# S5 tap masks as one VectorE product per window, with a changed order of the mixer's work

## Chip, cores and metric

One core of one Trainium2 chip runs the whole program in one launch. The metric is the device time of that launch in microseconds (us), and the median of several runs is compared. TensorE is the matmul engine, VectorE and ScalarE are the two elementwise engines, GpSimd is the slower general one, and SyncE issues most of the DMAs. In the profile they are called PE, DVE, ACT, POOL and SP.

## What is computed

One inference step of a hybrid decoder layer for 256 prompt tokens and 8 samples of 8 tokens (320 token columns in all, T = 320). The mixer at the layer's start has two halves that share one input projection: an S5 state-space group (512 channels, here "u") and an RWKV-7 group (the projections r, k, v and z, 512 channels each). After it come cross-attention and a top-4-of-32 mixture of experts. The change touches the S5 half alone:

```python
def s5_mixer(u, h0_re, h0_im, lam_re, lam_im, log_dt, b_re, b_im, c_re, c_im, d, glu_w, glu_b):
    dt = jnp.exp(log_dt.astype(f32))[:, None]
    mag = jnp.exp(lr * dt)
    ar = mag * jnp.cos(li * dt)
    ai = mag * jnp.sin(li * dt)
    ...
    bu_r = jnp.einsum('btgc,gpc->btgp', uf, bbar_r)
    bu_i = jnp.einsum('btgc,gpc->btgp', uf, bbar_i)
    acc_r, acc_i, x_r, x_i = lax.associative_scan(_complex_affine_combine, (a_r, a_i, bu_r, bu_i), axis=1)
    ...
    y = (jnp.einsum('gcp,btgp->btgc', c_re.astype(f32), x_r)
         - jnp.einsum('gcp,btgp->btgc', c_im.astype(f32), x_i)
         + d.astype(f32).reshape(S5_NGROUPS, S5_GROUP) * uf)
    z = jax.nn.gelu(y)
    out = z * jax.nn.sigmoid(z @ glu_w.astype(f32) + glu_b.astype(f32))
```

## The kernel before, in words

The recurrence is cut into blocks of BL = 8 tokens (40 blocks in 320 columns). The 512 S5 channels are handled in four tiles of 128 channels, numbered 0 to 3, and each tile goes through the same steps:

- **load** (`load_windows`, ScalarE's DMA queue): eight DMAs of 160 KB, one for each tap, gather shifted copies of u from DRAM into a window buffer of 128 x 2560 numbers (8 taps of 16 channels on the partitions, 8 groups of 320 columns along them). There are two buffers, for the even and the odd tiles. From tile 2 on, the load waits for the block matmuls of the tile two before.
- **win** (`mask_windows`, L1408 to L1413): a tap that reaches back beyond the start of its block of 8 has to be zero. ScalarE multiplies the window in place, one instruction for each of 7 column positions of the block, each 128 x 320 elements with a mask column as its scale.
- **f**, **par** (`f_matrices`, `s5_params`): the input matrices, made on VectorE for tiles 0 and 1 and on GpSimd for tiles 2 and 3 (L1701 to L1706, six products), then transposed by TensorE (L742) and multiplied to a kernel matrix (L746, L747), and copied out by ScalarE (L1350, L1397, L1398). GpSimd's six products for tile n+2 wait until TensorE has done `kk` of tile n+1, and they stand behind its own scan and start steps of tile n.
- **blk** (`s5_block`): TensorE's two jobs on the masked window, the block ends (L760) and the local part (L767). It waits for the masks (semaphore `uwin`).
- **scan** (L1894 to L1905, VectorE), after ScalarE has copied the block ends. GpSimd then forms the start state of every block (L1716 to L1726, the last of them signals `s5_x0`).
- **y** (L1909), **c** (L1879 to L1883, the output matrices; two rounds of two products and two halves), **out** (`s5_out`, L779 on TensorE, waits for the start states and the output matrices), **gelu** (L1914 to L1917; the first of the three frees the PSUM bank of `out`) and **gated** (L1922).

Between these steps TensorE computes the 16 tiles of the RWKV input projection (**in** k0 to v3, L716, 16 passes of 128x320 for a tile with two of them in each 1 MB weight chunk), and VectorE the token-shift mixing of them: **mix** (L1835 to L1844), **delta** and **shares** for z. Weight chunks for these tiles come over SyncE's queue into three slots in turn (L557). A chunk's load starts when TensorE has finished the last job that read the slot's former chunk: the chunk of r2 and r3 is requested when z1 is done.

The order of all that is a list written out by hand, `MIX_ORDER`. Every engine walks through the same list and does the steps that are its own, in that order, so a step waits on its own engine for everything ahead of it. PSUM banks go round by eight over the jobs in list order.

Of the kernel before, what the change touches and what calls it, by code (L numbers as in the profile page):

```python
# [25 lines left out]
ACT = mybir.ActivationFunctionType  # L26
# [11 lines left out]
BL = 8  # L38
# [137 lines left out]
def _tiles(kind, name, lo, hi):  # L176
# [2 lines left out]

IN_ORDER = "kzrv"  # L180
MIX_ORDER = [("in", "k0"), ("memsum", 0), ("load", 0), ("in", "k1"), ("f", 0), ("in", "k2"), ("load", 1), ("c", 0), ("in", "k3"),
             ("par", 0), ("memtotal", 0), ("win", 0), ("in", "z0"), ("f", 1), ("blk", 0), ("scan", 0), ("y", 0), ("in", "z1"), ("load", 2),
             ("memroot", 0), ("mix", "k"), ("in", "z2"), ("win", 1), ("out", 0), ("par", 1), ("in", "z3"), ("c", 1), ("blk", 1), ("gelu", 0),
             ("scan", 1), ("gated", 0), ("y", 1), ("in", "r0"), ("load", 3), ("delta", "z"), ("in", "r1"), ("shares", 0), ("shares", 1),
             ("out", 1), ("par", 2), ("c", 2), ("in", "r2"), ("win", 2), ("blk", 2), ("shares", 2), ("scan", 2), ("y", 2), ("gelu", 1),
             ("gated", 1), ("in", "r3"), ("in", "v0"), ("mix", "r"), ("out", 2), ("par", 3), ("in", "v1"), ("win", 3), ("c", 3), ("gelu", 2),
             ("gated", 2), ("blk", 3), ("scan", 3), ("y", 3), ("lora_up", 0), ("in", "v2"), ("in", "v3"), ("kk", 0), ("memnorm", 0),
             ("out", 3), ("gelu", 3), ("mix", "v"), ("gated", 3), ("lora_down", 0), ("knorm", 0), ("decays", 0), ("memk", 0),
             ("decay_exp", 0), ("memk", 1), ("memk", 2), ("memk", 3), ("memk", 4), ("memk", 5), ("glu", 0)]
TILES4 = range(4)  # L190


# [133 lines left out]
def build(nc, a, o):  # L326

    with ExitStack() as ctx:
# [5 lines left out]
        def S(name):  # L334
            if name not in sems:
                sems[name] = ctx.enter_context(nc.semaphore(name))
            return sems[name]
# [15 lines left out]
        def con(name, lo=0, hi=P):  # L353
            at, n = CON[name]
            return BIG[lo:hi, CONO + at:CONO + at + n]
# [11 lines left out]
        def over(ap, axis, n):  # L367

            v = ap.unsqueeze(axis)
            shape = list(v.shape)  # L370
            shape[axis] = n
            return v.to_broadcast(shape)
# [307 lines left out]
        def _(pe):  # L680
# [68 lines left out]

            def s5_block(ct):  # L750

                pe.wait_ge(S("uwin"), (BL - 1) * (ct + 1))
                uwin = uwins[ct % 2]
                stored(pe, f"ei{ct}")
                b = start_job(f"ve{ct}")
                for q in range(PAIRS):
                    for g in range(2):
                        for ri, e in ((0, E_r), (1, E_i)):
                            at = (ri * PAIRS + q) * NBL
                            last = mm(b[64 * g:64 * g + 64, at:at + NBL], e[:, q, 64 * g:64 * g + 64],  # L760
                                      uwin[:, 2 * q + g, BL - 1::BL], start=True, stop=True)
                end_job(last, f"ve{ct}")
                stored(pe, f"kk{ct}")
                b = start_job(f"loc{ct}")
                for g in range(2):
                    for q in range(PAIRS):
                        last = mm(b[32 * q:32 * q + 32, 0:T], kkz[:, 2 * q + g, :], uwin[:, 2 * q + g, :],  # L767
                                  start=(g == 0), stop=(g == 1))
                end_job(last, f"loc{ct}")
# [575 lines left out]
        def _(act):  # L1345
# [59 lines left out]
                    src = bass.AP(u_dram, ct * P * (T + 7) + tap, [[T + 7, GC], [GC * (T + 7), 8], [1, T]])  # L1405
                    act.dma_start(uwins[ct % 2][tap * GC:(tap + 1) * GC], src).then_inc(S(f"uwin_in{ct % 2}"), 16)

            def mask_windows(ct):  # L1408

                act.wait_ge(S(f"uwin_in{ct % 2}"), 16 * BL * (ct // 2 + 1))  # L1410
                w = uwins[ct % 2].rearrange("p g t -> p (g t)")
                for j in range(BL - 1):
                    step(af(w[:, j::BL], w[:, j::BL], ACT.Identity, scale=con("window")[:, j:j + 1]), "uwin")  # L1413

            act.wait_ge(S("u_stored"), 16)
            act.wait_ge(S("consts_in"), 16)
            for kind, n in MIX_ORDER:
                if kind == "in":
                    copy(prj[n[0]][:, int(n[1]), :], n)
                elif kind == "par":  # L1420
                    s5_params(n)
                elif kind == "load":
                    load_windows(n)
                elif kind == "win":
                    mask_windows(n)
                elif kind == "memsum":
                    norm_parts(rm, "m")
                elif kind == "memroot":
                    norm_roots(rm, "m", "rm")
                elif kind == "blk":  # L1430
                    if n >= 2:
                        act.wait_ge(S("s5_x0"), n - 1)
                    else:
                        act.wait_ge(S("s5_tables"), 1)
                    copy(xes[n % 2], f"ve{n}", lambda b: b[:, 0:2 * PAIRS * NBL].rearrange("p (r q n) -> p r q n", r=2, q=PAIRS))
                elif kind == "gelu":
                    act.wait_ge(S("gelu_arg"), n + 1)
                    step(af(mix[:, n, :], mix[:, n, :], ACT.Tanh, scale=float(np.sqrt(2 / np.pi))), "gelu_tanh")
                elif kind == "lora_up":
                    for job, dst, rows, fn in (("lw", hidden["dw"], 64, ACT.Tanh), ("la", hidden["da"], 64, ACT.Identity),  # L1440
                                               ("lg", hidden["dg"], P, ACT.Sigmoid)):
                        b = computed(act, job)
                        step.read_out(af(dst[0:rows, :], b[0:rows, 0:T], fn), job)
                elif kind == "lora_down":
                    for i in TILES4:
                        b = computed(act, f"dw{i}")
                        step.read_out(af(R[3][:, i, :], b[:, 0:T], ACT.Sigmoid, bias=vec("rwkv_w0", i)), f"dw{i}")
                    act.wait_ge(S("delta_free"), 1)
                    for i in TILES4:
                        b = computed(act, f"da{i}")  # L1450
                        step.read_out(af(R[7][:, i, :], b[:, 0:T], ACT.Sigmoid, bias=vec("rwkv_a0", i)), f"da{i}")
                    for i in TILES4:
                        copy(R[5][:, i, :], f"dg{i}")
                elif kind == "decay_exp":
                    act.wait_ge(S("decay_sums"), 1)
                    step(af(R[12], R[13], ACT.Exp, scale=-DECAY), "decay_exps")
                    step(af(R[9], R[13], ACT.Exp, scale=DECAY), "decay_exps")
                elif kind == "memk":
                    copy(mkT[:, n, :], f"mk{n}", lambda b: b[:, 0:NM])
                elif kind == "knorm":  # L1460
                    stored(act, "kn3")
                    inverse_root(R[15], R[15], 1.0, None, "kk_norm")
                elif kind == "glu":
                    for i in TILES4:
                        b = computed(act, f"gl{i}")
                        step.read_out(af(view(UWIN, CT, T)[:, i, :], b[:, 0:T], ACT.Sigmoid, scale=0.5, bias=vec("s5_glu_b", i)), f"gl{i}")
# [270 lines left out]
        def _(dve):  # L1737
# [147 lines left out]
            def scan_blocks(ct):  # L1885
# [18 lines left out]
                step(tt(xp[:, 0], xp[:, 0], turned[:, 0], sub))  # L1904
                step(tt(xp[:, 1], xp[:, 1], turned[:, 1], add), "s5_scanned")  # L1905

            def s5_local(ct):
                b = computed(dve, f"loc{ct}")
                step.read_out(stt(yl[ct], uT[:, ct, 7:], vec("s5_d", ct), b[:, 0:T], mul, add), f"loc{ct}")  # L1909
# [74 lines left out]
            for kind, n in MIX_ORDER:  # L1984
                if kind == "mix":
                    mixes(n)
                elif kind == "delta":
                    delta(n)
                elif kind == "shares":
                    share("z", R[4 + n], 3 + n)  # L1990
                elif kind == "memnorm":
                    mem_norm()
                elif kind == "f":
                    f_matrices(n)
                elif kind == "c":
                    c_matrices(n)
                elif kind == "y":
                    s5_local(n)
                elif kind == "scan":
                    scan_blocks(n)  # L2000
                elif kind == "gelu":
                    s5_gelu(n)
                elif kind == "gated":
                    s5_gated(n)
                elif kind == "kk":
                    kk_squares()
                elif kind == "decays":
                    decays()
# [368 lines left out]
```

## Time and profile before

| | us |
|---|---|
| median of 3 runs | 1464.74 |
| lowest and highest of them | 1461.38, 1467.27 |
| the profiled execution: its time | 1463.18 |
| the profiled execution: its span, first to last instruction | 1461.4 |
| TensorE busy | 1372.5 |
| VectorE busy | 436.1 |
| ScalarE busy | 266.0 |
| GpSimd busy | 54.6 |

The span is the stretch that every view of the trace covers, with its zero at the first instruction. The stretch of the S5 tiles and the projections lies at the start of it, from 29 us to about 176 us; the RWKV part and the attention follow, and the expert stage runs from about 520 us to the end. In the timeline a row is a run of equal instructions of one engine: start, duration to the end of the last, engine, line, operation, tiles, count, and in brackets the idle time before it with what ended it.

### The profile page before, as it was taken

How to read it: one execution, taken by the hardware profiler on the slowest of the kernel's cores; microseconds unless marked ns; L12 is line 12 of the kernel's file. 1: busy time of each engine (PE TensorE's matmuls, PEld its weight loads, DVE VectorE, ACT ScalarE, POOL GpSimd, SP SyncE). 2: the span in 40 equal slices, each digit the busy share in tenths (PEclk: the TensorE clock that was granted, in tenths of full speed). 3: DMA queues.
4: the chain of work that ended last, by engine and by line, in shares of the span. 5: the costliest groups of instructions: out<-in, count | busy, mean ns of one | idle time of the engine just before them, and what ended most of it. 6: DMA issues, size and time to landing. Idle time of an engine off the chain costs nothing.

```text
span 1461.4 us, 21175 instructions
## 1 busy us (share of the span) xinstructions
PE 1372.5 (94%) x8649; PEld 695.2 (48%) x8649; DVE 436.1 (30%) x879; ACT 266.0 (18%) x494; POOL 54.6 (4%) x111
## 2 busy tenths in 40 slices
PE   8796999999999999999999999998998999988997
PEld 5564688866665633434334343343343433433442
DVE  5787746435121221312112111121121111311112
ACT  4344331212223112101101011011010110110102
POOL 4342000000000000000000000000000000000000
PEclk9898999999999999999999999999999999999999
DMA  8871021013839679999999999999999999999994
GB/s 324 159 158 60 30 93 60 32 59 120 353 140 409 277 264 398 404 424 427 428 427 428 428 428 428 428 427 429 428 427 429 428 428 428 429 427 427 426 426 166
DMA packets 43335, 471.84 MB, mean 323 GB/s; under 512 B 4992, under 2 KB 10368, under 8 KB 11520
## 3 DMA queue, kind: packets, MB, share of 16 engines
q1 hardware_dynamic: 37264, 461.42, 76.1%
q10 hardware_dynamic: 6000, 9.41, 3.3%
q8 instruction: 52, 0.85, 0.2%
q14 instruction: 19, 0.16, 0.0%
HBM read 465.33 MB, written 5.48 MB: 322 GB/s over the span
## 4 chain that ended last, share of the span: by engine, by line
PE 71%; DMA 20%; DVE 4%; ACT 3%; issue 2%; ACTq 1%; SPq 0%; DVEq 0%
DMA big<-in_w_gu 18%; PE bank L1186 16%; PE bank L1235 14%; PE bank L716 9%; PE bank L1109 5%; PE bank L796 2%; PE bank L976 2%; PE bank L1299 2%; PE bank L1255 2%; ACT big L1413 2%; PE bank L895 1%; DMA big<-u_windows 1%; PE bank L1116 1%; PE bank L1211 1%; PE bank L1284 1%
## 5 line engine op out<-in xcount | busy, mean ns | idle before, releaser
L1186 PE MATMUL bank<-big 128*64 128x512 f32 x1920 | 427.9, 602 | 28.3 <-DMA big<-in_w_gu 27.3
L1186 PEld LDWEIGHTS bank<-big 128*64 128x64 f32 x1920 | 147.0, 138 | 306.1 <-issue 295.8
L1235 PE MATMUL bank<-big 128*64 128x512 f32 x960 | 209.4, 594 | 0.0
L716 PE MATMUL bank<-big 128*128 128x320 f32 (+1 forms) x688 | 187.8, 430 | 3.1 <-ACT big L1521 1.3
L716 PEld LDWEIGHTS bank<-big 128*128 128x128 f32 x688 | 130.1, 191 | 58.0 <-issue 8.1
L2232 DVE TENSOR_TENSOR big<-big,bank 128x320 f32<-128x320 f32 x120 | 58.5, 487 | 304.2 <-PE bank L1255 298.9
L2218 DVE TENSOR_SCALAR big<-bank 128x512 f32<-128x512 f32 x32 | 22.2, 693 | 392.5 <-PE bank L1186 362.3
L1235 PEld LDWEIGHTS bank<-big 128*64 128x64 f32 x960 | 69.9, 137 | 128.2 <-issue 126.5
L1590 ACT ACTIVATE big<-big 128x512 f32<-128x512 f32 x30 | 18.8, 626 | 449.3 <-DVE big L2218 449.3
L1350 ACT ACTIVATE big<-bank 128x320 f32<-128x320 f32 (+3 forms) x122 | 53.2, 436 | 222.9 <-PE bank L716 45.4
L1109 PE MATMUL bank<-big 128*128 128x512 f32 x192 | 85.4, 593 | 1.4 <-DVE big L2166 1.4
L1255 PE MATMUL bank<-big 128*128 128x320 f32 x240 | 68.9, 439 | 0.0
L1255 PEld LDWEIGHTS bank<-big 128*128 128x128 f32 x240 | 44.1, 189 | 28.9 <-issue 12.2
L1109 PEld LDWEIGHTS bank<-big 128*128 128x128 f32 x192 | 35.0, 189 | 40.2 <-issue 40.2
L1608 ACT ACTIVATE big<-bank 128x512 f32<-128x512 f32 x30 | 18.0, 599 | 189.8 <-PE bank L1235 189.8
L796 PE MATMUL bank<-big 128*128 128x256 f32 x128 | 42.3, 432 | 3.9 <-DVE big L2059 1.8
L976 PE MATMUL bank<-big 128*128 128x320 f32 x128 | 34.7, 432 | 0.0
L1573 ACT ACTIVATE big<-bank 128x512 f32<-128x512 f32 x32 | 19.0, 598 | 63.6 <-PE bank L1109 63.6
L760 PE MATMUL bank<-big 128*64 128x40 f32 x128 | 7.3, 296 | 24.2 <-ACT big L1413 22.7
L976 PEld LDWEIGHTS bank<-big 128*128 128x128 f32 x128 | 24.2, 189 | 10.3
L1299 PE MATMUL bank<-big 128*64 128x512 f32 x128 | 28.3, 594 | 0.0
L1413 ACT ACTIVATE big<-big 128x320 f32<-128x320 f32 x28 | 24.5, 874 | 7.7 <-DMA big<-u_windows 6.8
(407 smaller groups left out, 1162.1 us busy)
## 6 DMA issues: line engine op xcount, KB each, us to landing
big<-in_w_gu SPq DMA_DIRECT2D x128, 2048.0 KB, 25.1
big<-in_w_down SPq DMA_DIRECT2D x62, 2048.0 KB, 22.3
big<-in_dense SPq DMA_DIRECT2D x47, 1024.0 KB, 7.9
big<-u_windows ACTq DMA_DIRECT2D x32, 160.0 KB, 10.3
big<-in_w_down SPq DMA_DIRECT2D x4, 1024.0 KB, 19.5
big<-in_smw SPq DMA_DIRECT2D x1, 1408.0 KB, 19.7
big<-in_xT SPq DMA_DIRECT2D x2, 640.0 KB, 4.7
big<-in_consts SPq DMA_DIRECT2D x1, 1028.5 KB, 14.8
```

The lines of the kernel that those rows point to most:

```text
L716: last = mm(b[:, 0:n], w[:, k, :], src[:, k, :], start=(k == 0), stop=(k == kt - 1))
L796: ins = mm(b[:, 0:256], memT[:, k, t * P:(t + 1) * P], chunk(FIRST["memv"] + q, KT, 256)[:, k, :], start=(k == 0), stop=(k == KT - 1))
L976: last = mm(b[:, 0:T], w[:, k, :], mix[:, k, :], start=(k == 0), stop=(k == KT - 1))
L1109: last = mm(ps[5 + h][:, :], sel[:, t, :], htok[:, t, h * 512:h * 512 + 512], start=(t == 0), stop=(t == TT - 1))
L1186: last = mm(ps[n][part, :], xte[:, 2 * j + k, part], w[s][:, k, n * 512:n * 512 + 512], start=False, stop=end)
L1235: last = mm(ps[bank][part, :], actT[:, 4 * d + i, part], w[s][:, i, h * 512:h * 512 + 512], start=(d == 0 and i == 0), stop=end)
L1255: mm(ps[bank][:, 0:T], yb[:, n * P:(n + 1) * P], gtt, start=not first, stop=True).then_inc(psum_full[bank], 1)
L1299: last = mm(ps[n][part, :], xte[:, 2 * j + k, part], w[s][:, k, n * 512:n * 512 + 512], start=False, stop=end)
L1350: step.read_out(af(dst, b[:, 0:T] if src is None else src(b), ACT.Identity), job)
L1413: step(af(w[:, j::BL], w[:, j::BL], ACT.Identity, scale=con("window")[:, j:j + 1]), "uwin")
L2218: ts(hg, ps[h][:, :], LIMIT, None, ALU.min).then_inc(psum_free[h], 1)
L2232: tt(xT[:, i, :], xT[:, i, :], ps[bank][:, 0:T], add).then_inc(psum_free[bank], 1)
```

## The change

The masks leave ScalarE. VectorE now does one product for each tile's window, over all 8 column positions (128 x 2560 elements), with the mask row of 320 columns read again for each of the 8 groups. `uwin` counts one for a tile where it counted seven. The list gets a new order: both z0 and z1 stand ahead of the first block, and the masks of tiles 0 and 1 stand together there; the root of the memory norm (`memroot`) and the load of tile 2's window stand behind the first block's jobs; z3 and par 1 stand ahead of out 0; load 3 stands behind block 1; the third share of z moves behind gated 1, and the mask of tile 3 stands behind it, ahead of mix r.

```diff
-MIX_ORDER = [... ("par", 0), ("memtotal", 0), ("win", 0), ("in", "z0"), ("f", 1), ("blk", 0), ("scan", 0), ("y", 0), ("in", "z1"), ("load", 2),
-             ("memroot", 0), ("mix", "k"), ("in", "z2"), ("win", 1), ("out", 0), ("par", 1), ("in", "z3"), ("c", 1), ("blk", 1), ("gelu", 0), ...]
+MIX_ORDER = [... ("par", 0), ("memtotal", 0), ("in", "z0"), ("f", 1), ("in", "z1"), ("win", 0), ("win", 1), ("blk", 0), ("memroot", 0), ("load", 2), ("scan", 0),
+             ("y", 0), ("in", "z2"), ("mix", "k"), ("par", 1), ("in", "z3"), ("out", 0), ("c", 1), ("blk", 1), ("load", 3), ("gelu", 0), ...]
...
             def s5_block(ct):
-                pe.wait_ge(S("uwin"), (BL - 1) * (ct + 1))
+                pe.wait_ge(S("uwin"), ct + 1)
...
-            def mask_windows(ct):
-                act.wait_ge(S(f"uwin_in{ct % 2}"), 16 * BL * (ct // 2 + 1))
-                w = uwins[ct % 2].rearrange("p g t -> p (g t)")
-                for j in range(BL - 1):
-                    step(af(w[:, j::BL], w[:, j::BL], ACT.Identity, scale=con("window")[:, j:j + 1]), "uwin")
...
+            def mask_windows(ct):
+                dve.wait_ge(S(f"uwin_in{ct % 2}"), 16 * BL * (ct // 2 + 1))
+                step(tt(uwins[ct % 2], uwins[ct % 2], over(con("window"), 1, 8), mul), "uwin")
```

How the order stands on the engines. First TensorE around the first block of the S5 tiles (L716 is a projection tile by 8 passes, L760 and L767 the block, L742 to L747 par, L779 out). Before, from the end of the memory norm's sums:

```order
L710 MATMUL bank<-big 128x256
L716 MATMUL bank<-big 128x320 x8
L760 MATMUL bank<-big 64x40 x16
L767 MATMUL bank<-big 32x320 x8
L716 MATMUL bank<-big 128x320 x16
L779 MATMUL bank<-big 32x40 x64
L742 MATMUL bank<-big 128x128 x8
```

and with the change, at the same place:

```order
L710 MATMUL bank<-big 128x256
L716 MATMUL bank<-big 128x320 x16
L760 MATMUL bank<-big 64x40 x16
L767 MATMUL bank<-big 32x320 x8
L716 MATMUL bank<-big 128x320 x8
L742 MATMUL bank<-big 128x128 x8
```

So z1 stands ahead of block 0, and par 1 behind z2. Then, on the same engine, from the end of par 1 on:

```order
L747 MATMUL bank<-big 128x32
L716 MATMUL bank<-big 128x320 x8
L779 MATMUL bank<-big 32x40 x64
L760 MATMUL bank<-big 64x40 x16
L767 MATMUL bank<-big 32x320 x8
L716 MATMUL bank<-big 128x320 x16
```

Here z3, out 0 and block 1 follow each other; before, out 0 stood ahead of par 1 and z3.

VectorE behind the input matrices of tile 1 (L1866 before and L1857 now are the last of them; the scan begins at L1894 before and at L1885 now). Before:

```order
L1865 TENSOR_TENSOR big<-big 128x512
L1866 TENSOR_TENSOR big<-big 128x512
L1894 TENSOR_TENSOR big<-big 128x256
L1895 TENSOR_TENSOR big<-big 128x128
L1896 TENSOR_TENSOR big<-big 128x128
```

and with the change:

```order
L1856 TENSOR_TENSOR big<-big 128x512
L1857 TENSOR_TENSOR big<-big 128x512
L1901 TENSOR_TENSOR big<-big 128x2560 x2
L1885 TENSOR_TENSOR big<-big 128x256
L1886 TENSOR_TENSOR big<-big 128x128
```

Both masks, of tile 0 and of tile 1, stand ahead of the scan of tile 0.

VectorE ahead of the scan of tile 2, with the change (L1870 to L1874 are the output matrices of tile 2, with one row of them left out above):

```order
L1870 TENSOR_TENSOR big<-big 128x512
L1871 TENSOR_TENSOR big<-big 128x512
L1874 TENSOR_TENSOR big<-big 64x32x16 x2
L1901 TENSOR_TENSOR big<-big 128x2560
L1885 TENSOR_TENSOR big<-big 128x256
```

The mask of tile 2 stands behind all the output matrices of tile 2, and TensorE's block 2 waits for it.

## Rows read from the trace of the kernel before

**Rows 1.** The page: busy time, share of the span, instructions of each engine.
```profile
PE 1372.5 (94%) x8649; PEld 695.2 (48%) x8649; DVE 436.1 (30%) x879; ACT 266.0 (18%) x494; POOL 54.6 (4%) x111
```
**Rows 2.** Waits of TensorE from 50 to 176 us: total, times, longest.
```profile
PE bank L760 <- ACT big L1413: 22.7, 3, 8.9
```
**Rows 3.** Timeline of TensorE: the four blocks, the outs and the projections.
```profile
62.97 1.96 PE L760 MATMUL bank<-big 128*64 128x40 f32 x32 [8.88 <-ACT big L1413]
...
76.51 1.38 PE L779 MATMUL bank<-big 128*32 128x40 f32 x128
...
89.31 1.42 PE L760 MATMUL bank<-big 128*64 128x40 f32 x32 [1.48 <-issue]
90.66 1.28 PE L767 MATMUL bank<-big 128*32 128x320 f32 x16
...
100.71 1.38 PE L779 MATMUL bank<-big 128*32 128x40 f32 x128
...
116.16 1.96 PE L760 MATMUL bank<-big 128*64 128x40 f32 x32 [6.94 <-ACT big L1413]
...
133.79 4.57 PE L716 MATMUL bank<-big 128*128 128x320 f32 x16
145.25 1.96 PE L760 MATMUL bank<-big 128*64 128x40 f32 x32 [6.89 <-ACT big L1413]
...
149.43 7.22 PE L808 MATMUL bank<-big 128*64 128x320 f32 x24
```
**Rows 4.** TensorE in block 0: stretch, length, busy, granted clock, DMA share, GB/s.
```profile
63.00:68.00 5.00, 5.00 (x50) 0.50 0.73 88
```
**Rows 5.** Window DMAs: tile 1's eight; first DMA of tile 2 (72.8 us), 3 (97.0).
```profile
L1406 ACTq DMA_DIRECT2D big<-u_windows x8: 310/453/659, 42.9 to 46.6; - x8
...
DMA to landing us min/median/max: 17.1/19.6/21.3
...
DMA to landing us min/median/max: 6.8/6.8/6.8
...
DMA to landing us min/median/max: 3.3/3.3/3.3
```
**Rows 6.** The 1 MB weight chunk of r2 and r3, issued at 72.3 us.
```profile
DMA to landing us min/median/max: 6.1/6.1/6.1
```
**Rows 7.** Timeline of VectorE: scans, output matrices of tile 2, and a long product.
```profile
65.58 0.59 DVE L1894 TENSOR_TENSOR big<-big 128x256 f32<-128x256 f32 x1 [9.26 <-ACT big L1350]
...
73.74 2.31 DVE L1844 SCALAR_TENSOR_TENSOR big<-big 128x320 f32<-128x320 f32 x4
...
91.39 0.60 DVE L1894 TENSOR_TENSOR big<-big 128x256 f32<-128x256 f32 x1 [3.23 <-ACT big L1350]
...
96.52 0.49 DVE L1922 SCALAR_TENSOR_TENSOR big<-big 128x320 f32<-128x320 f32 x1
...
104.80 0.69 DVE L1879 TENSOR_TENSOR big<-big 128x512 f32<-128x512 f32 x1
...
111.73 1.48 DVE L1880 TENSOR_TENSOR big<-big 128x512 f32<-128x512 f32 x1
...
115.64 2.31 DVE L1844 SCALAR_TENSOR_TENSOR big<-big 128x320 f32<-128x320 f32 x4
...
127.47 0.19 DVE L1835 COPY big<-big 128x36 f32<-128x36 f32 x1
...
132.18 0.69 DVE L1879 TENSOR_TENSOR big<-big 128x512 f32<-128x512 f32 x1
...
137.98 0.73 DVE L1914 TENSOR_TENSOR big<-big,bank 128x320 f32<-128x320 f32 x1
...
158.45 1.49 DVE L1930 TENSOR_TENSOR big<-big 128x1280 f32<-128x1280 f32 x1
```
**Rows 8.** Timeline of GpSimd: hand-over of tile 0, and tile 3's six products.
```profile
71.65 1.35 POOL L1726 COPY big<-big 128x248 f32<-128x248 f32 x1
...
112.74 1.60 POOL L1706 TENSOR_TENSOR big<-big 128x512 f32<-128x512 f32 x1
```

More of the change, by code:

```diff
@@ L181 @@
 MIX_ORDER = [("in", "k0"), ("memsum", 0), ("load", 0), ("in", "k1"), ("f", 0), ("in", "k2"), ("load", 1), ("c", 0), ("in", "k3"),
[L182 to L189, printed above, removed]
+             ("par", 0), ("memtotal", 0), ("in", "z0"), ("f", 1), ("in", "z1"), ("win", 0), ("win", 1), ("blk", 0), ("memroot", 0), ("load", 2), ("scan", 0),
+             ("y", 0), ("in", "z2"), ("mix", "k"), ("par", 1), ("in", "z3"), ("out", 0), ("c", 1), ("blk", 1), ("load", 3),
+             ("gelu", 0), ("scan", 1), ("gated", 0), ("y", 1), ("in", "r0"), ("delta", "z"), ("in", "r1"), ("shares", 0),
+             ("shares", 1), ("out", 1), ("par", 2), ("c", 2), ("win", 2), ("in", "r2"), ("blk", 2), ("scan", 2), ("y", 2), ("gelu", 1), ("gated", 1),
+             ("shares", 2), ("in", "r3"), ("in", "v0"), ("win", 3), ("mix", "r"), ("out", 2), ("par", 3), ("in", "v1"), ("c", 3), ("gelu", 2), ("gated", 2),
+             ("blk", 3), ("scan", 3), ("y", 3), ("lora_up", 0), ("in", "v2"), ("in", "v3"), ("kk", 0), ("memnorm", 0), ("out", 3),
+             ("gelu", 3), ("mix", "v"), ("gated", 3), ("lora_down", 0), ("knorm", 0), ("decays", 0), ("memk", 0), ("decay_exp", 0),
+             ("memk", 1), ("memk", 2), ("memk", 3), ("memk", 4), ("memk", 5), ("glu", 0)]
 TILES4 = range(4)
@@ L1423, in _ @@
                     load_windows(n)
-                elif kind == "win":
-                    mask_windows(n)
                 elif kind == "memsum":
@@ L1994, in _ @@
                     f_matrices(n)
+                elif kind == "win":
+                    mask_windows(n)
                 elif kind == "c":
```

## The prediction

> **What bounds the kernel now.** I read the page first, then the chain of waits, the waits of TensorE, and last the timelines of TensorE, VectorE and GpSimd next to each other. TensorE is busy for 94% of the span [rows 1], so what can be won is mostly what it waits. In the stretch of the S5 tiles it waits in front of the matmuls of L760 for ScalarE's masks: 22.7 us in three waits [rows 2], which the timeline shows as 8.88, 6.94 and 6.89 us ahead of blocks 0, 2 and 3; ahead of block 1 it is 1.48 us [rows 3]. The 24.2 us of these four waits are all that the change can remove directly. Behind a wait TensorE also runs slower: in block 0 the granted clock is 0.50, that is 1.2 GHz, after an idle stretch of nearly 9 us [rows 4], and L760 takes 1.96 us there against 1.42 us in block 1, which had stood behind a short wait [rows 3].
>
> What lies behind this stretch goes by TensorE's progress: weight slots are refilled, and the expert weights first requested, when TensorE is through with what was in them. So I let a shift of TensorE at the end of the stretch (the start of the LoRA and last projections, at 149.43 us [rows 3]) pass to the end one for one.
>
> **Step 1, block 0.** z1 now fills the first wait. TensorE was free from 54.09 us (62.97 less 8.88 [rows 3]); one projection tile takes 4.57 us [rows 3], so z1 ends at 58.6. The mask of tile 0 starts where ScalarE's did, seven instructions and 6.3 us ahead of 62.97, at 56.7. Its price: no row has a product of 2560 elements. The nearest is one of 1280 elements of two SBUF inputs at 1.49 us [rows 7]; twice that, 3.0, is a little too much since a part of it is fixed, and I take 2.8. Bounds: 1.5 (as cheap as half its size) and 5.9 (twice 1.49 times 1.48/0.69, the ratio that a product of 512 elements shows when GpSimd works beside it against alone [rows 7]). Block 0 starts at 59.5 and takes 1.42 + 1.28 = 2.7 us [rows 3] at the full clock. With z2, par 1 (2.6 us, between L779 and L716 in the timeline) and z3, TensorE is at 74 us where it was at 87.8 before (89.31 less 1.48 [rows 3]). That is a lead of nearly 14 us, and if nothing else waited the change would be a clear gain.
>
> **Step 2, the second mask holds the first scan.** VectorE now has the mask of tile 1 ahead of the scan of tile 0. The last window DMA of tile 1 was issued at 46.6 and took 21.3 us, so it lands at 67.9 [rows 5]. Before, the scan began at 65.58 [rows 7]; ScalarE took up that mask only later, so nobody waited for the landing. And it gets later: z1 now ends at 58.6, so the 1 MB chunk of r2 and r3 is requested then, in the middle of tile 1's landings (60.0 to 67.9), and not at 72.3. The trace has the same meeting once: the chunk issued at 72.3 landed in 6.1 us [rows 6], and the first window DMA of tile 2, issued 0.5 us behind it, took 6.8 us, where that of tile 3, alone, took 3.3 [rows 5]. The difference, 3.5 us, is my value; bounds are 0 (the windows go first) and 6.1 (the chunk goes first as a whole). The mask of tile 1 can start at 71.4 and ends at 74.2.
>
> The page "DMA: Bandwidth & Descriptors" of the Trainium skill (section on queues, rings and completion order) says that each DMA engine goes round its queues packet by packet, which speaks against this change: the two queues share, and the windows lose what the chunk takes. By that rule the whole chunk counts, as in the two rows above; a rule of first come first served would leave the landing at 67.9.
>
> **Step 3, out 0 and out 1.** Scan 0 took 5.1 us (65.58 to 70.70) and GpSimd handed over 2.3 us later (end of L1726 at 73.00 [rows 8]). So: 74.2 + 5.1 + 2.3 = 81.6 for out 0, where it was 76.51 [rows 3]. TensorE's lead is gone, and it idles for over 7 us there. VectorE then has y 0 and mix k (70.70 to 76.05, 5.35 us [rows 7]), c 1 (5.8: 132.18 to 137.98 [rows 7]) and gelu 0 (1.8), 13.0 in all. GpSimd's six products for tile 2 fall on them, from 81.6 on. What that costs: the same six for tile 3 ended at 114.3 [rows 8], and c 2 beside them lasted from 104.80 to 115.64, 10.8 us against 5.8 alone [rows 7], a loss of 5.0. Before, those of tile 2 fell partly on an idle VectorE (its 3.23 us of waiting ahead of 91.39 [rows 7]) and cost it 2.6. I take 4.5 (bounds 2.6 and 5.0). Scan 1 starts at 79.3 + 13.0 + 4.5 = 96.8 (before 91.39) and ends at 101.9; with GpSimd's hand-over (1.4 us in its timeline for tile 1) out 1 starts at 103.3, before 100.71 [rows 3].
>
> **Step 4, block 2.** From the end of scan 1 VectorE has gated 0, y 1, delta and two shares (96.52 to 104.80, 8.3 us [rows 7]), c 2 (5.8 and again 4.5) and then the mask of tile 2, 2.8. Block 2 starts at 101.9 + 8.3 + 10.3 + 2.8 = 123.3. Before it was 116.16 [rows 3]. **VectorE, not the masks' own time, is the bound here, and this costs 7.1 us.**
>
> **Step 5, block 3.** From block 2 to the end of v1 it was 138.36 - 116.16 = 22.2 us [rows 3]; so v1 ends at 145.5. VectorE is through with gelu 1, gated 1, the third share (2.3) and the mask of tile 3 (2.8) some 16.4 us after the start of block 2 (gated 1 ended 11.3 us after it, since mix r began at 127.47 [rows 7]). So that mask waits for nobody, and the wait of 6.89 us [rows 3] is gone. Block 3 starts at 145.5 against 145.25, and it runs at the full clock: 2.7 us against 149.43 - 145.25 = 4.2 [rows 3], 1.5 less. The LoRA jobs lose their slow beginning (0.3 less), but the second of them needs the bank that gelu 2 frees, behind mix r (4.7) and c 3 (5.8): 0.4 us of waiting.
>
> **Sum:** +5.1 at out 0, +7.1 at block 2, then -6.9 for the wait at block 3, -1.5 and -0.3 for the clock, +0.4 for the bank; out 0's figure is inside block 2's. 7.1 - 6.9 - 1.5 - 0.3 + 0.4 = -1.2, rounded to -1. At nothing I cost ScalarE's relief (25 us of masks less; it was waited for through the masks alone), the issue of 8 DMAs ahead of z2's copy (TensorE waits at out 0 by then) and the earlier `memroot`. If VectorE were not the cover, ScalarE's 4.7 us of issues would be next. The profiled execution took 1463.18, so 1462.2 for one like it; it lies 1.6 below the median of 1464.74, and the median to expect is 1463.7.
>
> **Rivals.**
> - The windows keep their landing at 67.9. Every step up to block 2 is 3.5 us earlier and so is the end: -4.5, 1460.2. For it: these DMAs are in the queue 12 us ahead of the chunk. Against: tile 2's first DMA. Chance 0.23.
> - VectorE loses less to GpSimd (2.6 in each place, as at tile 2 before) and the landing stays: -4.5 - 3.8 = -8.3, and with cheap masks (1.5) 1.3 more at each of the two that lie on the path: -11, 1454. For it: with VectorE never idle GpSimd may be the one that waits. The page "SBUF — State Buffer" (who interferes with whom) says that the port both share is held for a whole instruction, whichever starts first. By that rule a long product makes GpSimd wait; the 0.69 that became 1.48 [rows 7] shows VectorE as the loser here. Chance 0.12.
> - Slower: the chunk is served wholly ahead of tile 1's last DMAs, 6.1 us instead of 3.5. The place is the same landing, and each us passes to the end; above a landing at 72.6 the change loses. At 74.0, and with 5.0 us lost to GpSimd twice, it gives -1.2 + 2.6 + 1.0 = +2.4, 1467.1. Chance 0.15. If also the products cost 5.9 (3.1 more at each of the two on the path), it is +8.6, 1473. Chance 0.05.
> - The change does not do what it says (masks still on ScalarE): the order shows four products of 128x2560 on VectorE and no L1413 left. No chance given.
> - The forecast itself, from -3 to +1: 0.45.
>
> **How the numbers follow.** A measurement of this kernel can tell about 0.5% from no change, that is 7.3 us. Faster by more (below 1457.4) is most of the second rival: 0.10. Slower by more (above 1472.1) is the case of dear products: 0.05. The rest, 0.85, is no change. The range takes the first rival and the slower one whole and most of the way to the second, and the runs of before themselves spread by 6 us: 1457.5 to 1469.
>
> **What would show it.** Right: VectorE waits for u_windows ahead of the second L1901, until about 71; scan 0 (L1885) starts near 74; TensorE waits at L779 for GpSimd's L1717 twice, 7 to 8 us each, and at block 2 for L1901; no wait at block 3; L1901 takes 2.8 us; LoRA (L808) starts near 148.5. Wrong: the second window landing at 68 (first rival); L1901 above 4 us; c 1 and c 2 short of 8 us each (second rival); or L808 at a place that the end does not follow, which would fell the one-for-one rule.

## The result and the profile after

The change makes the kernel a little slower: 1466.19 us median of 20 runs (1464.17 to 1470.11) against 1463.22 of 20 runs of the kernel before. The ratio is 1.0017, with a 95% interval of 1.001 to 1.0024, so the loss is 1.5 to 3.5 us. The time lies inside the range and within the 0.5% of no change, but with the other sign: I had forecast 1 us less. The profiled execution took 1465.37 us over a span of 1463.6, which is 2.2 us more than the span before.

The page of the kernel after, busy time [rows 1]:

```profile
span 1463.6 us, 21151 instructions
PE 1378.1 (94%) x8649; PEld 700.7 (48%) x8649; DVE 450.5 (31%) x883; ACT 241.3 (16%) x466; POOL 54.8 (4%) x111
```

ScalarE has lost 25 us of work and VectorE has gained 14. ScalarE's relief gains nothing beyond the masks: TensorE's other waits for it in this stretch were 0.9 and 0.5 us.

TensorE's waits from 50 to 176 us, in total, times and longest [rows 2]:

```profile
PE bank L779 <- issue: 11.1, 2, 6.6
PE bank L760 <- DVE big L1901: 9.3, 2, 6.0
PE bank L808 <- DVE big L1910: 0.6, 1, 0.6
```

Before, there were four waits of 24.2 us ahead of the blocks: three for the masks (22.7 us) and one of 1.48 us, which ended with ScalarE's copy of tile 1's input matrices (L1350, until 89.21), a copy that stood behind the masks. Now two waits of 9.3 us are for the masks and two of 11.1 us for the start states ahead of the outs (L779; the release, GpSimd's L1717 behind VectorE's scan, is not named but ends where they end). So 14.9 us of waiting ahead of the blocks went, and 11.7 came back as waits for other steps of the engine that now masks, VectorE (0.6 of it for gelu 2's bank).

The timeline of TensorE [rows 3], with start, duration and idle time before:

```profile
61.27 1.96 PE L760 MATMUL bank<-big 128*64 128x40 f32 x32 [3.33 <-DVE big L1901]
...
82.41 2.36 PE L779 MATMUL bank<-big 128*32 128x40 f32 x128 [4.48 <-issue]
...
105.80 2.36 PE L779 MATMUL bank<-big 128*32 128x40 f32 x128 [6.62 <-issue]
...
126.33 1.95 PE L760 MATMUL bank<-big 128*64 128x40 f32 x32 [5.97 <-DVE big L1901]
...
148.60 1.43 PE L760 MATMUL bank<-big 128*64 128x40 f32 x32
...
151.17 2.37 PE L808 MATMUL bank<-big 128*64 128x320 f32 x8
154.15 4.72 PE L808 MATMUL bank<-big 128*64 128x320 f32 x16 [0.62 <-DVE big L1910]
```

| start of, us | before | predicted | after |
|---|---|---|---|
| block 0 | 62.97 | 59.5 | 61.27 |
| out 0 | 76.51 | 81.6 | 82.41 |
| out 1 | 100.71 | 103.3 | 105.80 |
| block 2 | 116.16 | 123.3 | 126.33 |
| block 3 | 145.25 | 145.5 | 148.60 |
| LoRA jobs | 149.43 | 148.5 | 151.17 |

The LoRA jobs start 1.7 us late and end 2.2 us late, with the 0.62 us of the bank, and the span is 2.2 us longer: here the one-for-one rule holds to the tenth.

The timeline of VectorE [rows 7]: the two masks, scan 0, mix k in its contended part, scan 1, c 2 and the mask of tile 2.

```profile
58.39 2.83 DVE L1901 TENSOR_TENSOR big<-big 128x2560 f32<-128x2560 f32 x1 [2.53 <-DMA big<-u_windows]
73.05 2.82 DVE L1901 TENSOR_TENSOR big<-big 128x2560 f32<-128x2560 f32 x1 [11.83 <-DMA big<-u_windows]
75.91 0.60 DVE L1885 TENSOR_TENSOR big<-big 128x256 f32<-128x256 f32 x1
...
85.88 5.68 DVE L1835 SCALAR_TENSOR_TENSOR big<-big 128x320 f32<-128x320 f32 x4
...
99.22 0.59 DVE L1885 TENSOR_TENSOR big<-big 128x256 f32<-128x256 f32 x1
...
112.62 0.69 DVE L1870 TENSOR_TENSOR big<-big 128x512 f32<-128x512 f32 x1
...
123.45 2.83 DVE L1901 TENSOR_TENSOR big<-big 128x2560 f32<-128x2560 f32 x1
```

VectorE stands still for 11.83 us, with scan 0 behind the mask that it waits for, and from 73.05 to the block 2 it is never idle. The product costs 2.83 us where nothing else is at work.

The DMAs of tile 1's window [rows 5], the weight chunk [rows 6] and the first DMA of tile 2's window, in the kernel after. The first pair of lines is the last two window DMAs (issued 45.9 and 46.5), the second the chunk of r2 and r3, the third tile 2's first:

```profile
L1406 ACTq DMA_DIRECT2D big<-u_windows x2: 477/485/493, 45.9 to 46.5; - x2
DMA to landing us min/median/max: 21.4/23.9/26.5
...
L557 SPq DMA_DIRECT2D big<-in_dense x1: 328/328/328, 58.0 to 58.0; - x1
DMA to landing us min/median/max: 13.9/13.9/13.9
...
L1406 ACTq DMA_DIRECT2D big<-u_windows x1: 309/309/309, 67.3 to 67.3; - x1
DMA to landing us min/median/max: 5.3/5.3/5.3
```

The last but one lands at 45.9 + 21.4 = 67.3, 0.2 us later than before; the last at 46.5 + 26.5 = 73.0, and before at 67.9. So with the chunk requested at 58.0, as foretold, the window is complete 5.1 us later, though nearly all of it keeps its pace.

These landings need care in reading. The eight DMAs count on one semaphore, 16 counts each (`16 * BL`), and the view gives every 16 counts to the next DMA in the order of issue. By the semaphore's updates in the trace 126 of the window's 128 counts are there at 68.36, and the last two come at 70.76 and 72.96; before, the last two came at 67.85 and 67.91. What is late is 2 of 128 parts, and the trace does not say of which DMA.

### The profile page after: what moved, and what is told of

Its sections match the earlier page's. It is cut to its first block, busy times and chain, and to the rows that moved or that the text cites. A ratio compares the mean times of both kernels' runs of the same rounds, so it can differ in the third digit from the quotient of the medians.

```text
span 1463.6 us, 21151 instructions
## 1 busy us (share of the span) xinstructions
PE 1378.1 (94%) x8649; PEld 700.7 (48%) x8649; DVE 450.5 (31%) x883; ACT 241.3 (16%) x466; POOL 54.8 (4%) x111
## 4 chain that ended last, share of the span: by engine, by line
PE 68%; DMA 20%; DVE 9%; issue 1%; ACT 1%; ACTq 0%; SPq 0%; DVEq 0%
DMA big<-in_w_gu 18%; PE bank L1186 16%; PE bank L1235 14%; PE bank L716 9%; PE bank L1109 5%; PE bank L976 2%; PE bank L796 2%; PE bank L1299 2%; PE bank L1255 2%; DMA big<-u_windows 2%; PE bank L895 1%; DVE big L1835 1%; PE bank L1116 1%; PE bank L1211 1%; PE bank L1284 1%
## 5 line engine op out<-in xcount | busy, mean ns | idle before, releaser
L716 PE MATMUL bank<-big 128*128 128x320 f32 (+1 forms) x688 | 190.7, 435 | 2.2 <-ACT big L1512 1.3
L716 PEld LDWEIGHTS bank<-big 128*128 128x128 f32 x688 | 132.3, 194 | 58.7 <-issue 9.9
L2216 DVE TENSOR_SCALAR big<-bank 128x512 f32<-128x512 f32 x32 | 22.2, 693 | 392.2 <-PE bank L1186 362.1
L1350 ACT ACTIVATE big<-bank 128x320 f32<-128x320 f32 (+3 forms) x122 | 53.1, 436 | 247.1 <-PE bank L716 49.3
L976 PEld LDWEIGHTS bank<-big 128*128 128x128 f32 x128 | 24.2, 189 | 10.3
L2223 DVE TENSOR_TENSOR big<-big 128x512 f32<-128x512 f32 x32 | 22.2, 695 | 10.3 <-ACT big L1581 6.4
L1123 PE MATMUL bank<-big 32*128 32x512 f32 x128 | 19.2, 671 | 6.1 <-issue 6.1
## 6 DMA issues: line engine op xcount, KB each, us to landing
big<-in_w_down SPq DMA_DIRECT2D x62, 2048.0 KB, 22.3
```

What stands on the lines that cost most here:

```text
L716: last = mm(b[:, 0:n], w[:, k, :], src[:, k, :], start=(k == 0), stop=(k == kt - 1))
L976: last = mm(b[:, 0:T], w[:, k, :], mix[:, k, :], start=(k == 0), stop=(k == KT - 1))
L1350: step.read_out(af(dst, b[:, 0:T] if src is None else src(b), ACT.Identity), job)
L2216: ts(hg, ps[h][:, :], LIMIT, None, ALU.min).then_inc(psum_free[h], 1)
L2223: tt(hact[:, h * 512:h * 512 + 512], hu, sig, mul).then_inc(S("activated"), 1)
```

## The experiments

Two theories stood against each other. **A, the order:** the loss comes from VectorE's scan of tile 0 (and with it everything up to block 2) standing behind the landing of tile 1's window, and the landing is late through the weight chunk. **B, the load:** VectorE has no room for four more products, wherever they stand. All ratios are to the kernel before, as is "faster" where nothing else is said.

### The masks alone, in the order of before

```diff
-MIX_ORDER = [... as in the change]
+MIX_ORDER = [... as before the change]
```

> The masks as one VectorE product each, in the order of before (win 0 ahead of z0, win 1 behind z2). Theory A (the loss comes from the order, which puts VectorE's scan of tile 0 behind the landing of tile 1's window): the scan of tile 0 starts near 61 us as soon as block 0 is copied, no window mask waits for more than a few us of landing except the first, TensorE waits at no mask but the first and the third, and the program is 6 to 9 us faster than before. Theory B (VectorE is too full for the masks, wherever they stand: 4 times 2.83 us of products on an engine that already bounds the stretch): no faster than before, 0 to +3 us.

Measured: 1457.21 us, ratio 0.9946 (0.993 to 0.9963), 5 to 10 us faster. In its timeline TensorE waits for masks ahead of blocks 0 and 2 alone (9.08 and 11.76 us), and the LoRA jobs start at 144.22. The part that was a miss: scan 0 starts at 67.11, not near 61, since in this order f 1 stands between the mask of tile 0 and the scan, and that mask waited for a landing at 59.8. B falls: the same four products on VectorE make a clear gain.

### The order alone, with the masks on ScalarE

```diff
-            def mask_windows(ct):
-                dve.wait_ge(S(f"uwin_in{ct % 2}"), 16 * BL * (ct // 2 + 1))
-                step(tt(uwins[ct % 2], uwins[ct % 2], over(con("window"), 1, 8), mul), "uwin")
...
+            def mask_windows(ct):
+                act.wait_ge(S(f"uwin_in{ct % 2}"), 16 * BL * (ct // 2 + 1))
+                w = uwins[ct % 2].rearrange("p g t -> p (g t)")
+                for j in range(BL - 1):
+                    step(af(w[:, j::BL], w[:, j::BL], ACT.Identity, scale=con("window")[:, j:j + 1]), "uwin")
```

> The new order with the masks left on ScalarE, 7 instructions for a tile. Theory A: ScalarE now has the mask of tile 1, and so the landing of its window at 68 to 73 us, ahead of its copy of block 0 and of every later copy; the first scan starts only near 80 and out 0 near 88 to 91, and the blocks 2 and 3 make up part of it. The program ends 0 to 5 us slower than before. Theory B: the order by itself is good and the product on VectorE is what costs, so this run is faster than before by 3 us or more.

Measured: 1463.05 us, ratio 1.0 (0.999 to 1.0009), no change. The timeline of ScalarE shows the landing holding the next mask and the copy of block 0 behind it, and that of VectorE scan 0 waiting for that copy:

```profile
70.97 6.33 ACT L1413 ACTIVATE big<-big 128x320 f32<-128x320 f32 x7 [6.27 <-DMA big<-u_windows]
77.33 0.44 ACT L1350 ACTIVATE big<-bank 128x320 f32<-128x320 f32 x1
```

```profile
77.86 0.59 DVE L1894 TENSOR_TENSOR big<-big 128x256 f32<-128x256 f32 x1 [22.02 <-ACT big L1350]
```

So the order has a loss in it whichever engine masks, and gains that balance it. The masks alone save 8 us, the order alone nothing, and both together lose 2.5: the two parts are not additive. In the order of before, with the masks on VectorE, the mask of tile 1 starts at 77.64, over 10 us behind the landing of its window (67.2); there a late landing is free.

### The mask of tile 1 behind mix k

```diff
-("in", "z1"), ("win", 0), ("win", 1), ("blk", 0), ("memroot", 0), ("load", 2), ("scan", 0), ("y", 0), ("in", "z2"), ("mix", "k"), ("par", 1)
+("in", "z1"), ("win", 0), ("blk", 0), ("memroot", 0), ("load", 2), ("scan", 0), ("y", 0), ("in", "z2"), ("mix", "k"), ("win", 1), ("par", 1)
```

> The change, with the mask of tile 1 moved from ahead of scan 0 to behind mix k. Theory A: the scan of tile 0 starts near 63 us and not at 76, out 0 waits 1 to 2 us and not 4.5, out 1 comes near 96 and not 105.8, block 2 near 116 and not 126.3; the program is 8 to 11 us faster than the change, so 6 to 9 us faster than before. Theory B: within 2 us of the change, since the same four products are still on VectorE and only change places.

Measured: 1454.21 us, ratio 0.9944 (0.9931 to 0.9958), 6 to 10 us faster. One step moved in a list turns the loss into a gain. VectorE's timeline:

```profile
56.01 2.83 DVE L1901 TENSOR_TENSOR big<-big 128x2560 f32<-128x2560 f32 x1 [0.23 <-DMA big<-u_windows]
60.98 0.60 DVE L1885 TENSOR_TENSOR big<-big 128x256 f32<-128x256 f32 x1 [2.14 <-ACT big L1350]
...
75.54 3.77 DVE L1901 TENSOR_TENSOR big<-big 128x2560 f32<-128x2560 f32 x1
```

Scan 0 starts at 60.98 and not at 75.91, though the window of tile 1 again landed late, at 72.5. This product costs 3.77 us, 0.94 more than alone; the last of GpSimd's six products, from 75.24 to 76.63, was still running beside it. TensorE's waits, which show what comes next:

```profile
PE bank L760 <- DVE big L1901: 16.8, 3, 10.7
```

The 10.7 us are block 2's, whose mask stands behind c 2.

### The weight chunk held back

```diff
                 if PREV[c] is not None:
                     computed(sp, LAST_JOB[PREV[c]])
+                if c == 7:
+                    sp.wait_ge(S("uwin_in1"), 16 * BL)
```

> The change, with one wait more on SyncE: the 1 MB weight chunk of r2 and r3 is requested only when tile 1's window has landed. Theory A with the collision (the chunk requested at 58.0 us makes the last window DMA land at 73.0 and not at 68): it lands at 67.5 to 68.5, the second mask starts there, and the whole chain up to block 2 comes 4.5 to 5.5 us earlier: the program is 4 to 5.5 us faster than the change, 2 to 3 us faster than before. Rival: the late landing is a scatter of this one profile, or does not come from the chunk; then the landing stays at 71 to 74 or is at 68 in both, and the time is within 1 us of the change.

Measured: 1460.91 us, ratio 0.9984 (0.9973 to 0.9995); that is 5.3 us less than the change by the medians and 0.33% by the ratios, 4.8 us. The second mask starts at 66.49 instead of 73.05:

```profile
66.49 2.83 DVE L1903 TENSOR_TENSOR big<-big 128x2560 f32<-128x2560 f32 x1 [4.04 <-DMA big<-u_windows]
```

Block 2 starts at 119.35 instead of 126.33. The profiled execution was one of the fastest of the twelve (1458.55; they go from 1457.98 to 1464.97), so the 7 us of block 2 are more than the runs gain on average. The collision is no scatter of one profile. The landing can be read in all twelve kernels. The seven that request the chunk near 58 us have a late one, and the five that request it after 66 us have not:

| kernel | chunk of r2, r3 requested | chunk landed | tile 1's window landed |
|---|---|---|---|
| before | 72.3 | 78.4 | 67.9 |
| masks alone | 71.7 | 78.1 | 67.2 |
| one chunk held | 66.5 | 72.2 | 66.4 |
| both chunks held, order of the change (below) | 68.0 | 84.4 | 67.5 |
| both chunks held, last order (below) | 66.9 | 81.8 | 66.4 |
| order alone | 57.9 | 70.7 | 70.9 |
| mask products twice (below) | 58.8 | 71.3 | 71.6 |
| tile 1's mask moved | 57.9 | 71.5 | 72.5 |
| the change | 58.0 | 71.9 | 73.0 |
| masks 1 and 2 moved (below) | 58.9 | 72.5 | 74.0 |
| and c 2 moved (below) | 58.8 | 73.2 | 74.7 |
| GpSimd's products left out (below) | 59.3 | 73.7 | 75.7 |

In all seven late ones the window is complete 0.2 to 2.1 us behind the chunk, the later the chunk, the later the window. What is late are mainly the last two of its 128 counts: the last comes 1.9 to 5.4 us behind the 126th, and in the other five 0.3 to 0.7 us.

### Each mask product done twice

```diff
                 dve.wait_ge(S(f"uwin_in{ct % 2}"), 16 * BL * (ct // 2 + 1))
+                step(tt(uwins[ct % 2], uwins[ct % 2], over(con("window"), 1, 8), mul))
                 step(tt(uwins[ct % 2], uwins[ct % 2], over(con("window"), 1, 8), mul), "uwin")
```

> The change, with every mask product done twice (a mask of ones and zeros times itself, so nothing else changes): 2.83 us more at each of four places. If two of the four lie on the path (tiles 1 and 2), the first hides in the landing of tile 1's window and the fourth under the projections ahead of block 3, the program is 5 to 6.5 us slower than the change, block 2 comes 5.5 to 6 us later, and block 3's own mask still makes no wait. Rival: VectorE bounds the whole stretch, then all four count, and it is 9 to 12 us slower. Rival: the products hide in idle time, then it is under 2 us.

Measured: 1472.57 us, ratio 1.0053 (1.0037 to 1.0069): 6.4 us more than the change by the medians, 5.3 by the ratios. In the profile block 2 comes 4.4 us later; the landing was 1.3 us earlier in that execution, so two products' worth, 5.7, is in it. The mask of tile 1 stands behind the landing and that of tile 2 behind c 2, and both are on the path. The expectation for the fourth was wrong: block 3 indeed does not wait, but the second LoRA job, which has the bank that gelu 2 frees, waits 3.61 us and not 0.62.

```profile
161.40 6.25 PE L808 MATMUL bank<-big 128*64 128x320 f32 x16 [3.61 <-DVE big L1911]
```

### GpSimd's products left out

Five of the six products for the input matrices of tiles 2 and 3 are left out, and these matrices are not computed.

```diff
-                step(tt(fr, pr, br, ALU.mult))
-                step(tt(tmp, pi, bi, ALU.mult))
-                step(tt(fr, fr, tmp, ALU.subtract))
-                step(tt(fi, pr, bi, ALU.mult))
-                step(tt(tmp, pi, br, ALU.mult))
-                step(tt(fi, fi, tmp, ALU.add), "s5_f")
+                step(tt(fi, pr, bi, ALU.mult), "s5_f")
```

> The change, with five of GpSimd's six products left out for tiles 2 and 3 (their input matrices are then not computed), so that VectorE has its operands to itself. From the end of scan 0 to scan 1 VectorE took 18.2 us in the change against 13.0 of work, and from scan 1 to the mask of tile 2 19.1 against 14.1. If these 10 us are what GpSimd costs it: c 2 takes 6 to 6.5 us and not 10.8, block 2 comes 7.5 to 10 us earlier than in the change, and the program is 6 to 9 us faster than the change. Rival (VectorE loses the time to something else, as to the DMAs or to its own waits): within 2 us of the change.

Measured: 1459.43 us, ratio 0.9961 (0.9947 to 0.9976), 6.8 us less than the change by the medians. VectorE's c 2 now runs at its own pace; this is its second half, as far as the mask:

```profile
114.85 0.69 DVE L1865 TENSOR_TENSOR big<-big 128x512 f32<-128x512 f32 x1
115.58 0.69 DVE L1866 TENSOR_TENSOR big<-big 128x512 f32<-128x512 f32 x1
116.30 1.41 DVE L1869 TENSOR_TENSOR big<-big 64x512 f32<-64x512 f32 x2
117.75 2.83 DVE L1896 TENSOR_TENSOR big<-big 128x2560 f32<-128x2560 f32 x1
```

From scan 0's end to scan 1 VectorE takes 14.0 us and not 18.2 (83.8 to 97.8), from scan 1's end to the mask of tile 2 14.8 and not 19.1. The 8.5 us are what five products on GpSimd cost VectorE in two places, with one left in each. Block 2 starts only 5.7 us earlier than in the change because tile 1's window landed 2.8 us later (75.7).

### Masks of tiles 1 and 2 both moved

The mask of tile 1 as above, and that of tile 2 from behind c 2 to behind y 1. The second part as a diff:

```diff
-("gated", 0), ("y", 1), ("in", "r0"), ("delta", "z"), ("in", "r1"), ("shares", 0), ("shares", 1), ("out", 1), ("par", 2), ("c", 2), ("win", 2), ("in", "r2")
+("gated", 0), ("y", 1), ("win", 2), ("in", "r0"), ("delta", "z"), ("in", "r1"), ("shares", 0), ("shares", 1), ("out", 1), ("par", 2), ("c", 2), ("in", "r2")
```

> The change with the mask of tile 1 behind mix k and that of tile 2 right behind y 1, ahead of the z shares and of c 2 (its window has long landed). The 10.7 us wait ahead of block 2 that was left with tile 1's mask moved alone should go, down to under 1 us; v 0 then waits 5 to 7 us for the bank that gelu 1 frees, behind c 2. By the walk along the rows the gain over moving tile 1's mask alone is 1.5 to 2.5 us: 9.5 to 12 us faster than before. Rival: block 2's wait was the whole rest, then 8 us or more over moving tile 1's mask alone.

Measured: 1453.33 us, ratio 0.993 (0.9913 to 0.9947). The wait ahead of block 2 is gone, and reappears as foretold ahead of v 0, larger than expected (11.50 us and not 5 to 7), because the bank of out 1 is now free only behind the z shares, c 2 and the scan of tile 2:

```profile
122.42 6.99 PE L716 MATMUL bank<-big 128*128 128x320 f32 x16 [11.50 <-DVE big L1910]
```

Against tile 1's mask alone it is 0.9 us by the medians, which the intervals do not tell apart: the further gain of 1.5 to 2.5 us that was expected is not shown.

### And c 2 behind gelu 1

```diff
-("par", 2), ("c", 2), ("in", "r2"), ("blk", 2), ("scan", 2), ("y", 2), ("gelu", 1), ("gated", 1)
+("par", 2), ("in", "r2"), ("blk", 2), ("scan", 2), ("y", 2), ("gelu", 1), ("c", 2), ("gated", 1)
```

> As the kernel with both masks moved, and c 2 moved behind gelu 1, so that the bank of out 1 comes free before the output matrices of tile 2. v 0 no longer waits; out 2 waits for c 2 instead, a few us. 0.5 to 2 us faster than with both masks moved, 10 to 13 us faster than before. Rival: VectorE's sum of work bounds the stretch up to the LoRA jobs, so the order within it changes nothing: within 0.5 us of the kernel with both masks moved.

Measured: 1451.51 us, ratio 0.9918 (0.9898 to 0.9939), 9 to 15 us faster than before and the fastest of the study. The waits of TensorE from 50 to 170 us:

```profile
PE bank L760 <- DVE big L1901: 5.6, 2, 3.2
PE bank L716 <- DVE big L1910: 5.5, 1, 5.5
PE bank L808 <- DVE big L1910: 3.2, 1, 3.2
```

v 0 still waits, 5.5 us, where I had expected nothing, and out 2 does not wait, where I had expected a few us; the second LoRA job waits 3.2 us for gelu 2. The step over the run before is 1.8 us by the medians with intervals that overlap by far, so it is not shown, and the rival (no change within 0.5 us) stands.

### Both chunks held, with the order of the change and with the last one

```diff
                 if PREV[c] is not None:
                     computed(sp, LAST_JOB[PREV[c]])
+                if c == 6:
+                    sp.wait_ge(S("uwin_in1"), 16 * BL)
```

The second of the two kernels has this hold and the order of the run above, with the masks of tiles 1 and 2 and c 2 moved.

> The change, with the weight chunk of r0 and r1 (and behind it, in the queue's order, that of r2 and r3) requested only when tile 1's window has landed. If a 1 MB chunk costs the last window DMA it meets, both windows gain: tile 0's last lands near 55 us (58.3 in the change), tile 1's near 63 to 66 (73.0 in the change, 66.4 with only the chunk of r2 and r3 held), block 0 waits under 1.5 us, and block 2 starts 8 to 10 us earlier than in the change. The program is 6 to 9 us faster than the change, 1 to 4 us faster than with one chunk held. Rival: the windows need their 1.2 us for a DMA in any case, and tile 1's last stays at 66 to 68; then within 1 us of the kernel with one chunk held.

Measured: 1458.18 us, ratio 0.9961 (0.9947 to 0.9974). The rival's landing came for tile 1: 67.5, no earlier than with one chunk held, and block 2 starts at 120.88, even 1.5 us later than with one. Tile 0's window landed at 56.2, against 55.9 to 59.8 in the ten kernels that do not hold the chunk of r0 and r1. The time did what the expectation said: 8.0 us less than the change by the medians (8.2 by the ratios), and 2.7 us less than with one chunk held (3.4 by the ratios, intervals that barely touch). The two profiled executions do not show this gain (spans of 1457.0 and 1456.8; that of one chunk held was among the shortest of its twelve), so where it comes from stays open.

> The order with masks 1 and 2 and c 2 moved, with both chunks held as well. There VectorE takes up tile 1's mask only behind mix k (77.5 us), so its landing is off the path; only block 0 gains, 1 to 3 us, and out 0 behind it. 0.5 to 1.5 us faster than without the hold, 11 to 14 us faster than before. Rival: projection tile r0 then waits for its late chunk, and it is slower than without the hold.

Measured: 1451.91 us, ratio 0.9921 (0.9905 to 0.9937), the same as without the hold. As expected the landing is off the path there; block 0 starts at 58.79 and not at 61.98, and the small gain expected from that was not to be seen in the time.

## Why the prediction was right and wrong

- **One for one to the end:** right for the change. LoRA jobs end 2.2 us later, span 2.2 us longer. As a rule it is rougher: with tile 1's mask moved the LoRA jobs start 10.7 us earlier and the span is 11.4 shorter, but in the last kernel of all they start 16.9 us earlier and the span is 9.2 shorter, in part because the second of them waits 3.6 us there. Taken at out 3, behind these jobs, the shift and that of the span differ by up to 1.7 us in ten kernels and by 2.5 in the last.
- **Step 1, block 0:** the price of the product, 2.8 us, was right (2.83). The start was 1.7 us off, since the first window landed at 58.3 and not at 56.6; it lies between 55.6 and 59.8 over the profiles of this study. It cost nothing, because scan 0 waited for the second mask until 75.9.
- **Step 2, the second mask holds scan 0:** right in kind, and shown by moving that mask. **The term that failed in size is the delay of the landing:** I had put 3.5 us, read from the first DMA of tile 2's window. It is 5.1 us, 73.0 against 67.9 (6.6 against the 66.4 of the run with the chunk held). The window is not slowed as a whole: the last two of its 128 counts come at 70.76 and 72.96, around the chunk's own landing at 71.9. The prediction's own tipping point was a landing at 72.6, and the 1.65 us by which this term was short are by themselves enough to turn its gain of 1.2 into a loss.
- **Step 3:** out 0 came at 82.41 (81.6), the 1.65 us of the landing less 0.9 of GpSimd's hand-over, whose last copy took 0.40 us where it had taken 1.35. **GpSimd's toll on VectorE was the second term too small:** 4.5 us, measured 18.2 - 13.0 = 5.2 in the first place and 19.1 - 14.1 = 5.0 in the second. The bound of 5.0 was too low as well. That it is GpSimd's is shown by leaving its products out, and with it the rival falls in which VectorE loses only 2.6 in each place.
- **Step 4:** block 2 at 126.33 and not 123.3. The 3.0 us are 1.65 of the landing, 0.7 and 0.5 of GpSimd, and 0.2 of rounding.
- **Step 5:** right. From block 2 to block 3 it took 22.3 us (22.2), block 3 did not wait and ran at the full clock in 2.6 us (2.7), and the bank cost 0.6 us (0.4).
- **The sum:** -1.2 + 3.0 + 0.2 = +2.0 for the profiled execution, which showed +2.2. The rival that ends slower, the landing at 74.0 with GpSimd at its dear bound, was put at +2.4 with a chance of 0.15, and it is the one that came closest (a landing at 73.0, and 5.2 and 5.0 us to GpSimd). The forecast named the steps and had the direction of the end wrong, because in both places I took a kinder value than the trace offered; the time fell inside the range because the range was wide. The median of 1463.7 that I gave stood on the median of three runs, 1464.74; that of twenty is 1463.22.
- **Waits of 7 to 8 us at both outs:** 4.48 and 6.62. TensorE came later to them, because block 0 started 1.8 us late and because it ran slower: its granted clock was 0.50, 1.2 GHz, behind the wait at block 0 and behind that at out 0, where I had put block 0 at the full clock. Behind the wait at out 1 it was the same. These slow pieces fall into the next wait, where VectorE is the one waited for, and cost nothing more; in the busy time they show as 5.6 us for the same 8649 matmuls.

The granted clock of these stretches (length, busy, clock, DMA share, GB/s):

```profile
61.00:65.40 4.40, 4.13 (x48) 0.50 1.14 137
82.40:89.00 6.60, 6.52 (x176) 0.50 0.11 42
105.80:118.00 12.20, 12.20 (x161) 0.50 0.01 2
```

In the prediction I cited the page "DMA: Bandwidth & Descriptors" of the Trainium skill for queues that are served in turn by packet. The direction agrees with the table of landings above. That all DMAs in flight are slowed alike, which is how I read it, does not: 126 of the window's 128 counts came where they had, and the last two only at 70.76 and 72.96, around the chunk's landing at 71.9. For the page "SBUF — State Buffer" of the Trainium skill and its port that is held for a whole instruction, the 128x2560 product that met the end of one GpSimd product took 3.77 us against 2.83, and the 0.94 more is less than the 1.09 us which that product still ran, so it agrees. No run has the long product beside several of GpSimd's; my bound of 5.9 us was not reached in any.

The delay of 3 to 8 us over the seven kernels follows the chunk's own landing (70.7 to 73.7). What stays open is why just two counts are held until then: no view or run here tells the DMA engines apart.

## What to carry to other kernels

Work that moves to another engine takes its waits with it: ask for each moved step what stands behind it in that engine's order, and put a step that waits for a transfer as late as its own user allows. The same four products made 8 us of gain or 2.5 us of loss, depending on whether one of them stood behind or ahead of steps that did not need it. Where a faster engine asks for its next weights earlier, find what else is in flight at that time; one chunk requested 14 us earlier cost 5 us on a small transfer that the path waited for. And a landing read from a count that several DMAs share tells when all are in, but not which of them was late.

## What the runs showed of the hardware

- A 1 MB weight load on SyncE's queue that meets eight 160 KB gathers on ScalarE's queue leaves 126 of their 128 counts in their pace in the change (1.2 us for 16 of them, the 126th at 68.36; 67.1 to 71.7 in the seven kernels) and makes the last count 3 to 8 us late (70.9 to 75.7 against 67.9), always behind the load's own landing; the load takes 12.5 to 14.4 us in the seven kernels, against 6.1 before. In the change the first counts of gathers issued 21 us later on the same queue came (71.2) ahead of the last of these (73.0).
- Six GpSimd products of 128x512 cost a VectorE that is never idle 5.0 and 5.2 us, beside four shares of mix k (5.68 us against 2.31) as well as beside products.
